# A down projection by seven products: its sums of weight blocks built in DRAM by accumulating transfers, and one ring of eight staging buffers

## What is computed

```python
D_FF = ((8 * D_MODEL // 3 + 255) // 256) * 256      # 5632
...
h = rmsnorm(x, g_ffn[l])
u = causal_dwconv(h @ w_up[l], ffn_conv_w[l]) + ffn_conv_b[l]
gate, val = jnp.split(u, 2, axis=-1)
x = x + (jax.nn.silu(gate) * val) @ w_down[l]
return rmsnorm(x, g_final)
```

## Time and profile before

| | us |
|---|---|
| median of 3 runs (lowest, highest) | 1957.52 (1957.0, 1957.82) |
| the profiled execution, its own time | 1957.91 |
| its span | 1956.1 |
| TensorE busy | 1934.3 |
| VectorE busy | 1374.3 |
| ScalarE busy | 1049.1 |
| GpSimd busy | 47.1 |
| bytes moved by the DMA engines | 357.31 MB, 183 GB/s |
| of them on q1 (SyncE) | 349.35 MB, 57.5% of the 16 engines |
| of them on q0 (GpSimd) | 6.61 MB, 1.0% |
| mean granted clock of TensorE | 0.998 of full |

### The profile page before, as it was taken

The page is one execution under the profiler, slowest core; times in us unless marked ns, Lnnn a source line. Parts: engine busy times, 40 slices in busy tenths (PEclk is TensorE's granted clock), DMA queues, the critical chain, the costliest instruction groups (busy, mean ns, idle before and its releaser), DMA issues.

```text
span 1956.1 us, 28874 instructions
## 1 busy us (share of the span) xinstructions
PE 1934.3 (99%) x9826; PEld 1637.7 (84%) x9826; DVE 1374.3 (70%) x1948; ACT 1049.1 (54%) x1533; POOL 47.1 (2%) x74
## 2 busy tenths in 40 slices
PE   8999999999999999999999999999999999999997
PEld 7788888888788888888888888888888888888886
DVE  6655675665655676656668766888877887888787
ACT  5533576654433566664554544555555555555553
POOL 1000030000000011000100000000000000000000
PEclk9999999999999999999999999999999999999999
DMA  8666445545566546545666545566666566676663
GB/s 299 202 193 193 142 152 161 153 158 183 175 197 193 159 146 186 146 156 178 216 187 184 169 161 184 175 193 191 187 189 191 186 190 186 191 239 210 207 195 108
DMA packets 246727, 357.31 MB, mean 183 GB/s; under 512 B 15302, under 2 KB 136480, under 8 KB 246108
## 3 DMA queue, kind: packets, MB, share of 16 engines
q1 hardware_dynamic: 245004, 349.35, 57.5%
q0 software_dynamic: 1616, 6.61, 1.0%
HBM read 352.75 MB, written 3.16 MB: 182 GB/s over the span
## 4 chain that ended last, share of the span: by engine, by line
PE 95%; DVE 2%; ACT 1%; DMA 1%; issue 1%; SPq 0%; DVEq 0%; ACTq 0%
PE acc L410 21%; PE acc L387 15%; PE acc L389 15%; PE acc L388 15%; PE acc L403 11%; PE acc L1246 3%; PE acc L1245 3%; PE acc L1244 3%; PE aux L467 2%; PE aux L960 1%; PE aux L1246 1%; PE aux L1245 1%; PE aux L1244 1%; DVE sb_w_lo L350 1%; PE aux L978 1%
## 5 line engine op out<-in xcount | busy, mean ns | idle before, releaser
L350 DVE TENSOR_TENSOR sb_w_lo<-sb_stage,sb_w_hi 128x1024 fp32r<-128x1024 f32 x567 | 694.4, 1228 | 384.0 <-ACT sb_w_hi L345 373.0
L345 ACT ACTIVATE sb_w_hi<-sb_stage 128x1024 fp32r<-128x1024 f32 x567 | 598.4, 1058 | 492.2 <-PE acc L389 239.0
L410 PE MATMUL acc<-sb_xT,sb_w_hi 128*128 128x512 f32 x1856 | 445.7, 391 | 0.0
L410 PEld LDWEIGHTS acc<-sb_xT,sb_w_hi 128*128 128x128 f32 x1856 | 340.8, 188 | 65.8
L387 PE MATMUL acc<-sb_w_hi,sb_xT 128*128 128x512 f32 x768 | 306.2, 399 | 1.6 <-issue 1.6
L389 PE MATMUL acc<-sb_w_hi,sb_xT 128*128 128x512 f32 x768 | 299.6, 390 | 0.0
L388 PE MATMUL acc<-sb_w_lo,sb_xT 128*128 128x512 f32 x768 | 299.3, 390 | 0.0
L403 PEld LDWEIGHTS acc<-sb_xT,sb_w_lo 128*128 128x128 f32 x1856 | 238.7, 191 | 9.3
L403 PE MATMUL acc<-sb_xT,sb_w_lo 128*128 128x256 f32 x1856 | 243.0, 283 | 0.0
L387 PE MATMUL acc<-sb_w_hi,sb_mT 128*128 128x512 f32 x560 | 224.7, 401 | 1.3 <-issue 1.1
L389 PE MATMUL acc<-sb_w_hi,sb_mT 128*128 128x512 f32 x560 | 218.6, 390 | 0.0
(11 more groups left out here) (334 smaller groups left out, 1922.3 us busy)
## 6 DMA issues: line engine op xcount, KB each, us to landing
sb_stage<-w_in SPq DMA_DIRECT2D x248, 512.0 KB, 3.9
sb_stage<-w_up SPq DMA_DIRECT2D x176, 512.0 KB, 3.6
sb_stage<-w_out SPq DMA_DIRECT2D x96, 512.0 KB, 3.7
sb_stage<-w_down SPq DMA_DIRECT2D x60, 512.0 KB, 7.5
sb_pair_stage<-w_down SPq DMA_DIRECT2D x28, 512.0 KB, 7.1
sb_stage<-w_kv SPq DMA_DIRECT2D x16, 512.0 KB, 6.8
sb_stage<-w_ukv SPq DMA_DIRECT2D x16, 512.0 KB, 3.6
sb_stage<-w_uq SPq DMA_DIRECT2D x12, 512.0 KB, 3.6
```

The lines of the kernel that those rows point to most:

```text
L345: act.activation(w_hi[:, j % RING, 0:size], stage[:, j % RING, 0:size], ACT.Copy).then_inc(hi_ready, 1)
L350: dve.tensor_tensor(w_lo[:, j % RING, 0:size], stage[:, j % RING, 0:size], w_hi[:, j % RING, 0:size].bitcast(F32), ALU.subtract).then_inc( ...
L410: mm = pe.matmul(acc[:, 2 * pair + c, :], hi[:, k, c * P:(c + 1) * P], both, start=first and k == 0, stop=last and k == 3)
```

## The change

The four sums of the sevens are no longer made by VectorE. A DRAM tensor `down_sums` of 128 x 2 x 2 x 7 x 2 x 512 holds them for all 14 sevens. GpSimd builds it with sixteen transfers of 128 x 7 x 512 float32 (seven blocks at a time, 1.835 MB each), eight for each chunk of columns: four copies, then four transfers that add to what is there, with waits between those that depend on each other. They stand in GpSimd's program behind the pooling weights and ahead of the final gain.

All units of the down projection now use one ring of eight staging buffers: the four of `stage` and four of `stage_more`, which takes the place of `pair_stage` in memory. A seven is loaded as four units, `seven2` and `seven3` from `down_sums` (after a wait for all sums), and SyncE's loads are in the order of the units. The load of unit j waits until VectorE is through with unit j - 8; units 4 to 7 wait until TensorE is through with the up projection.

```diff
-DOWN_RING = 6
+DOWN_RING, DOWN_STAGES = 6, 8
...
+    sums_dram = nc.dram_tensor("down_sums", [P, 2, 2, SEVEN, 2, 512], F32, kind="Internal").ap()
...
-        pair_stage = sb("pair_stage", [P, 2, 2, UNIT], F32, down)
+        stage_more = sb("stage_more", [P, DOWN_STAGES - RING, UNIT], F32, down)
...
+        def blocks_of_pairs(k, c):
+
+            return bass.AP(tensor=dram["w_down_2"].tensor, offset=k * P * D + c * 512,
+                           ap=[[D, P], [2 * P * D, SEVEN], [1, 512]])
...
+        def down_stage(j):
+
+            s = j % DOWN_STAGES
+            return stage[:, s, :] if s < RING else stage_more[:, s - RING, :]
...
         def round_down(act, j):
...
-            if kind == "seven2":
-                act.wait_ge(sums_ready, 2 * n + 1)
-            if kind == "seven3":
-                act.wait_ge(sums_ready, 2 * n + 2)
+            act.wait_ge(*down_staged(j))
             act.wait_ge(unit_used, U4 + max(0, j - DOWN_RING + 1))
...
             dve.tensor_tensor(lo, src, hi.bitcast(F32), ALU.subtract).then_inc(lo_ready, 1)
-            if DOWN[j][0] == "seven1":
...
-                step(dve.tensor_tensor(b11, b11, b12, ALU.add))
-                dve.tensor_tensor(b12, b12, b22, ALU.add).then_inc(sums_ready, 1)
-                dve.wait_ge(sums_ready, 2 * sevens_until(j) - 1)
-                step(dve.tensor_tensor(b22, b11, b22, ALU.add))
-                dve.tensor_tensor(b21, b22, b21, ALU.add).then_inc(sums_ready, 1)
...
+                for j, (kind, i, c) in enumerate(DOWN):
+                    two = down_stage(j).rearrange("p (k n) -> p k n", n=512)
+                    if j < RING:
+                        sp.wait_ge(lo_ready, U4 + (j - RING + 1))
+                    elif j < DOWN_STAGES:
                         sp.wait_ge(unit_used, U4)
                     else:
+                        sp.wait_ge(lo_ready, U4 + (j - DOWN_STAGES + 1))
+                    if kind == "rows":
+                        load_ = sp.dma_start(two, w_down2[:, 2 * i:2 * i + 2, c * 512:(c + 1) * 512])
+                    if kind == "seven0":
+                        load_ = sp.dma_start(two, crossed(2 * i, 2 * c))
+                    if kind == "seven1":
+                        load_ = sp.dma_start(two[:, 0, :], w_down2[:, 2 * i + 1, 2 * c * 512:(2 * c + 1) * 512])
+                    if kind in ("seven2", "seven3"):
+                        sp.wait_ge(sums_done, 32)
+                        load_ = sp.dma_start(two, sums_dram[:, c, int(kind == "seven3"), i, :, :])
+                    load_.then_inc(down_staged(j)[0], 16)
...
+                for c in range(2):
+                    first_sum, second_sum = sums_dram[:, c, 0, :, 0, :], sums_dram[:, c, 0, :, 1, :]
+                    third_sum, all_sum = sums_dram[:, c, 1, :, 0, :], sums_dram[:, c, 1, :, 1, :]
+                    pool.dma_start(first_sum, blocks_of_pairs(0, 2 * c + 1)).then_inc(sums_copied, 16)
+                    pool.dma_start(second_sum, blocks_of_pairs(0, 2 * c + 1)).then_inc(sums_copied, 16)
+                    pool.dma_start(third_sum, blocks_of_pairs(1, 2 * c + 1)).then_inc(sums_copied, 16)
+                    pool.dma_start(all_sum, blocks_of_pairs(1, 2 * c)).then_inc(sums_copied, 16)
+                    pool.wait_ge(sums_copied, 64 * (c + 1))
+                    pool.dma_start(first_sum, blocks_of_pairs(0, 2 * c), accum_op=ALU.add).then_inc(sums_added, 16)
+                    pool.dma_start(second_sum, blocks_of_pairs(1, 2 * c + 1), accum_op=ALU.add).then_inc(sums_added, 16)
+                    pool.wait_ge(sums_added, 48 * c + 32)
+                    pool.dma_start(third_sum, first_sum, accum_op=ALU.add).then_inc(sums_added, 16)
+                    pool.wait_ge(sums_added, 48 * c + 48)
+                    pool.dma_start(all_sum, third_sum, accum_op=ALU.add).then_inc(sums_done, 16)
```

More of the change, by code:

```diff
@@ L148 @@
 SEVEN_FIRST = [j for j, unit in enumerate(DOWN) if unit[0] == "seven0"]
-DOWN_RING = 6
-def sevens_until(j):
-    return sum(first <= j for first in SEVEN_FIRST)
+DOWN_RING, DOWN_STAGES = 6, 8
 def prepared_at(u):
@@ L302, in build @@
         gate_conv, gate_silu, act_ready = sem("gate_conv"), sem("gate_silu"), sem("act_ready")
-        pair_staged = [sem("pair_staged0"), sem("pair_staged1")]
-        sums_ready, first_copied, seven_free = sem("sums_ready"), sem("first_copied"), sem("seven_free")
+        more_staged = [sem(f"more_staged{i}") for i in range(DOWN_STAGES - RING)]
+        first_copied, seven_free = sem("first_copied"), sem("seven_free")
+        sums_copied, sums_added, sums_done = sem("sums_copied"), sem("sums_added"), sem("sums_done")
         last_product = [sem("last_product0"), sem("last_product1")]
@@ L633, in build, with crossed @@
         SQ_PRO = 8
-        def crossed(k, c, side):
+        def crossed(k, c):
             return bass.AP(tensor=dram["w_down_2"].tensor, offset=k * P * D + c * 512,
-                           ap=[[D, P], [P * D + side * 512, 2], [1, 512]])
+                           ap=[[D, P], [P * D + 512, 2], [1, 512]])
+        def blocks_of_pairs(k, c):
+            return bass.AP(tensor=dram["w_down_2"].tensor, offset=k * P * D + c * 512,
+                           ap=[[D, P], [2 * P * D, SEVEN], [1, 512]])
         def down_slot(j):
@@ L647, in down_parts, with down_staged @@
         def down_parts(j):
-            kind = DOWN[j][0]
             hi, lo = down_slot(j)
[L651 to L659, removed]
-        def round_down(act, j):
[L663 to L668, removed]
-            if kind == "seven2":
-                act.wait_ge(sums_ready, 2 * n + 1)
-            if kind == "seven3":
-                act.wait_ge(sums_ready, 2 * n + 2)
+            n = 512 if DOWN[j][0] == "seven1" else UNIT
+            return down_stage(j)[:, 0:n], hi[:, 0:n], lo[:, 0:n]
+        def down_stage(j):
+            s = j % DOWN_STAGES
+            return stage[:, s, :] if s < RING else stage_more[:, s - RING, :]
+        def down_staged(j):
+            s, n = j % DOWN_STAGES, j // DOWN_STAGES + 1
+            return (staged[s], 16 * (U4 // RING + n)) if s < RING else (more_staged[s - RING], 16 * n)
+        def round_down(act, j):
+            act.wait_ge(*down_staged(j))
             act.wait_ge(unit_used, U4 + max(0, j - DOWN_RING + 1))
@@ L2152, in _ @@
                     for ahead in prepared_at(j):
-                        rest_down(step, dve, ahead)
+                        rest_down(dve, ahead)
                     if j == 0:
```

18 lines of the change are left out of this document (1 added, 17 removed).

## The result

The changed kernel takes 2017.76 us (median of 4, 2016.14 to 2020.21) beside 1957.26 us of the kernel before (4 runs, 1956.08 to 1957.82): ratio 1.031, 95% interval 1.030 to 1.032. It is 60.5 us slower. The profiled execution took 2020.21 us, its span is 2018.4.

What follows compares the result with a forecast made beforehand. TensorE was taken as the bound, busy 1934.3 of 1956.1 us. Packet turns cost 110.3 us, less 17 for pauses and starting lead, less 2.2 at the end: +91, so 2049 us, range 1975 to 2122.

Steps and rivals of the forecast that it cites:

- Where and how: TensorE idle only between about 970 and 1200 us, waiting for roundings that wait for w_in loads; down stage 230 us.
- The end: End of the down projection: the ring of eight gets the late load there in time; -2.2 us, at most 2.4.
- Sums off VectorE: Down projection: 38.8 us of VectorE work and ScalarE's waits for it go; worth nothing while loads keep ahead.
- first units: Ring's second half, loaded once TensorE is through the up projection: unit 4 due 10.9 us later, load 3.5 us; nothing.
- more bytes: Down stage: a seven and two row units need 283 GB/s where the queue moved 390; nothing, or a few us.
- The price of a packet: Engine time per 4 KB packet on GpSimd's queue: copy 0.246 us, add 0.328; 3584 packets per kind.
- Turns: From 967.4 us GpSimd's and the weight queue alternate by packet: 110.3 us lost in both halves; chance 0.60.
- the breaths: Six pauses between dependent transfers, in each 3 us the weights can take 0.98 MB; 14 us off the loss.
- The clock: A stalled TensorE may fall from 2.4 GHz towards 1.2: hidden while starved, in pauses it could take back 14 us.
- Shut out altogether: Rival: weights get nothing while GpSimd's queue has work; +109 us (2067), at dear prices 2122; chance 0.15.
- Only the copies crowd: Rival: adds leave the engines to others, only copies cost; +30 us (1988), with cheap copies +12 (1970); chance 0.13.
- Not slower: Rival: from 967 us the weight queue keeps 181 GB/s and TensorE never runs dry; 1955.7 us; chance 0.08.

Runs made afterwards that it cites:

- Run 2: Kernel before, with the sixteen transfers added at the same place on GpSimd's queue and their sums read by no one: 2021.89 us, ratio 1.0323.
- run 9: Kernel before, with only the last four units loaded into the two pair_stage buffers as soon as these are free: 1954.6 us, ratio 0.9987.
- run 1: Changed kernel without the sixteen transfers, plain blocks of w_down loaded in place of the sums: 1954.2 us, ratio 0.9984.
- run 7: Changed kernel, output complete, each of the sixteen transfers waiting until TensorE has used 16 more units, some 45 us apart: 1966.26 us, ratio 1.0047.
- run 5: Changed kernel without the eight adds, each copy waiting until the one before has landed: 1970.67 us, ratio 1.0069.
- run 3: Changed kernel with the eight adding transfers left out, the eight copies alone: 1988.61 us, ratio 1.0158.
- run 11: Changed kernel, output complete, eight copies and eight whole adds, the adds some 70 us apart, none at the start of mixing or up projection: 1966.11 us, ratio 1.0042.
- run 10: Changed kernel, output complete, eight copies and sixteen half adds 30 to 40 us apart from the first block on: 1954.23 us, ratio 0.9988.
- run 8: Changed kernel, output complete, copies 22 to 40 us apart, adds halved and 19 to 25 us apart, kept off stage starts: 1972.14 us, ratio 1.0074.

## Why the prediction was right in its sign and too dark in its size

*Where and how.* Right: TensorE idle (but for short waits that the kernel before has too) only between about 975 and 1205 us, at the end of a chain of loads, roundings and low parts; the loads' landing grown (3.5 us in the earlier trace rows; 17.6 in 995 to 1000); the down stage intact. Run 2 shows that the transfers alone do it.

*The end.* Forecast -2.2 us with at most 2.4; measured 12.1 - 9.4 = -2.7 in the spans, 2.3 in the medians of run 9, 3 in those of run 1. Mechanism and size were right, and the bound was a little too tight.

*Sums off VectorE, first units, more bytes.* Nothing each, as forecast (runs 1 and 9).

*The price of a packet.* The copy: 0.246 us forecast, 0.227 measured. The add: 0.328 for 4 KB forecast, 2 x 0.197 = 0.39 measured, but in packets of 2 KB. The condition that I had set, "near 3584 per kind", fails for the adds (7168 of data). In sum the two errors make the engines' time for the sixteen 142.5 us where 2 x 112 x (0.246 + 0.328) = 129 was forecast. The prediction had the case of 2 KB packets beside the sum ("If packets were 2 KB, the weights would get twice as many turns") and did not give it weight.

*Turns.* Both the earlier trace rows occur: the earlier trace rows for most of a burst, for the start of most bursts (not of all, run 7). The Trainium skill, "DMA: Bandwidth & Descriptors", under queues, rings and completion order, has each DMA engine go round its queues packet by packet. The middle of a burst agrees (375 packets against 313 in 1005 to 1010 us); the start of most bursts does not (no packet of the weights in the first 5 us of a copy in run 7), and there the measurement decides. I had to choose one of the two for the whole length and chose the one that carried more of it.

*The step that failed: the breaths.* I counted six, each of 3 us and 0.98 MB, only where the program waits for a transfer. What holds GpSimd back is how much can be out at once, two copies or one add, so there were eleven, and the thin ends of the bursts belong to them. In bytes: forecast were 4 x 1.84 = 7.4 MB by turns and 6 x 0.98 = 5.9 MB in breaths, in 170 us. The queue moved 28.87 MB in 231 us. At most 11008 packets of 1.08 KB, 11.9 MB, are turns; so at least 17 MB came in the breaths and thin ends, 1.5 MB for each of eleven. Of the 11 MB that the term was short, 5 x 0.98 = 4.9 MB are breaths not counted, and 6.2 MB are that each gave more than I put. The weights thus gained 4.5 + 11.1 = 15.6 MB, 89 us of TensorE at 176 GB/s, and the chain was 61 us longer: 28 us less loss. The forecast was too high by 2049 - 2017.8 = 31. Runs 5 and 3 show by experiment what breaths are worth: only their number differs, and the loss is 16.5 against 34 us. That the time fell inside the range owes something to errors of opposite sign: dearer transfers and shut-out starts on one side, more turns and far more breaths on the other.

*The clock.* The prediction let a lower clock take back the 14 us of the breaths. It is real (0.89 over the stretch, run 11), and most of the 23 us of longer busy time are its doing: busy time times the missing share of the clock, summed over the 46 windows of 5 us from 975 to 1205 us, is 19 us. How much of that a full clock would have saved in the starved stretch stays open: there the loads set the pace, and no run could hold the clock up. The byte count above, 67 us against 65 measured, leaves little for it.

*The rivals.* Shut out altogether (2067 and more) is refuted for the burst, true for the start of most. "Only the copies crowd" (1988) is refuted by run 3: without the adds it is 1988.61, with them 2017.76, so the adds cost some 29 us of their own. "Not slower" failed as the sixteen are issued, but it was the price of the order and not of the bytes: run 10 has the same bytes at 1954.23. Its condition, that no load may be held up for longer than the pipeline's lead, was the right one; I had put it to the whole chain and never to a single burst.

## What to carry to other kernels

A spare DMA share is spare only over the length of the lead that the loads hold: ask how long one burst is (from issue to landing 13 us for a single copy of 1.8 MB in run 5, 16 to 19 for an adding one in run 11, 10 to 13 for a half in run 10), and how long the loads then need to get ahead again (here 30 to 40 us from burst to burst were enough for halves and, ahead of the mixing stage, for whole copies; 19 to 26 were too few, and so were 33 to 35 for whole copies in the mixing stage, run 8), before summing bytes. If a transfer needed late can be issued early, cut it small and tie the pieces to the progress of the engine that must not starve; that turned 60 us of loss into none. And ask of a big change which part is worth anything: here it was four loads near the end, to be had in a few lines (run 9).

## What the hardware showed that I had not expected

- At the start of most bursts on GpSimd's queue SyncE's queue was shut out nearly or wholly (0 to 80 packets in 5 us), though both took turns one for one afterwards; some bursts had the turns from the start (181 packets against 221 in run 7).
- GpSimd stood for 16 to 21 us between transfers that the program lets go back to back: two copies or one add of 1.8 MB at a time.
- An adding transfer moves in packets of 2 KB where the copy of the same rows moves in 4 KB, and costs 89.8 against 52.7 us of the engines' time for eight; issued singly, eight adds cost TensorE some 29 us and eight copies 16.5.
- A stall of 2.66 us brought the granted clock to 0.52 in the next 5 us and 0.80 in those after, and cost twice its length (run 11).
